# Halving the weight split of one more unit, moving three output steps in a hand-written order, and cutting the first constants' transfer in two

## The reference

```python
n = rmsnorm(x, ln1)
rq, rk, rv, rg, gq, gk, gv, gg, ga, m_r, m_g = split_cols(n @ w_in)
o_r, s_ret = chunked_gated_linear(rotary(rq), rotary(rk) * RET_DK ** -0.5, rv, log_gamma, s_ret)
y_r = (group_rmsnorm(o_r, g_ret) * silu(rg)) @ w_ret_out
log_a = log_sigmoid(ga @ w_gate_up + b_gate_up) / 16
o_g, s_gla = chunked_gated_linear(gq * GLA_DK ** -0.5, gk, gv, log_a, s_gla)
y_g = (group_rmsnorm(o_g, g_gla) * silu(gg)) @ w_gla_out
h = x + (sigmoid(m_r) * y_r + sigmoid(m_g) * y_g) @ w_o
u, vv = split(rmsnorm(h, ln2) @ w_up)
h = h + (gelu(causal_dwconv(u)) * vv) @ w_down
y = rmsnorm(h, ln_f)
```

## Time and profile before

| | |
|---|---|
| median of 3 runs | 823.83 us (823.05, 823.83, 824.13) |
| profiled execution, its own time | 824.17 us |
| its span, from the first to the last instruction | 822.4 us |
| TensorE busy in the span | 812.3 us (99%) |
| VectorE busy | 588.8 us (72%) |
| ScalarE busy | 377.9 us (46%) |
| GpSimd busy | 218.4 us (27%) |
| mean granted TensorE clock | 0.996 of full speed |

### The profile page before, as it was taken

One profiled execution on the slowest core, in us unless ns is written; L12 is line 12 of the kernel. 1 busy time (PEld: TensorE's weight loads), 2 busy tenths in 40 slices (PEclk: granted clock), 3 DMA queues, 4 the chain that ended last, 5 costly groups with the idle time before them and its releaser, 6 DMA issues.

```text
span 822.4 us, 15722 instructions
## 1 busy us (share of the span) xinstructions
PE 812.3 (99%) x6522; PEld 798.8 (97%) x6522; DVE 588.8 (72%) x766; ACT 377.9 (46%) x535; POOL 218.4 (27%) x261
## 2 busy tenths in 40 slices
PE   9999999999999999999999999999999999999996
PEld 9989999999989999999999999999999999999996
DVE  5475669487899786766568877777777756778973
ACT  5653244322456363443244544443444424544574
POOL 4028247343427300000530333333322222000020
PEclk9999999999999999999999999999999999999998
DMA  9769968983328963537996686576677873765622
GB/s 272 220 206 173 270 215 182 202 263 103 110 80 149 231 234 97 186 130 231 199 271 195 142 259 202 150 203 202 241 184 202 231 172 103 202 181 172 175 60 108
DMA packets 163090, 152.32 MB, mean 185 GB/s; under 512 B 6710, under 2 KB 144682, under 8 KB 163005
## 3 DMA queue, kind: packets, MB, share of 16 engines
q1 hardware_dynamic: 129420, 109.73, 42.6%
q0 software_dynamic: 33440, 41.09, 26.6%
q10 hardware_dynamic: 160, 0.53, 0.2%
HBM read 145.36 MB, written 58.40 MB: 248 GB/s over the span
## 4 chain that ended last, share of the span: by engine, by line
PE 95%; DVE 3%; issue 1%; ACT 0%; DVEq 0%
PE mm L2063 52%; PE ax L2371 14%; PE mm L2485 8%; PE ax L2485 6%; PE ax L2084 6%; PE mm L2371 4%; PE ax L2089 2%; PE mm L2146 1%; PE mm L2084 1%; DVE grs L1478 1%; DVE wlo L1468 1%; DVE ysil L1725 0%; DVE ylo L1730 0%; DVE wlo L1742 0%; ACT whi L1030 0%
## 5 line engine op out<-in xcount | busy, mean ns | idle before, releaser
L2063 PE MATMUL mm<-nhi,whi 128*128 128x272 f32 x928 | 196.4, 293 | 0.5 <-DVE wlo L1468 0.5
L2063 PE MATMUL mm<-nhi,wlo 128*128 128x272 f32 x928 | 191.9, 288 | 0.0
L2063 PE MATMUL mm<-nlo,whi 128*128 128x272 f32 x928 | 191.4, 288 | 0.0
L1030 ACT ACTIVATE whi<-raw 128x1024 fp32r<-128x1024 f32 (+2 forms) x111 | 128.2, 1190 | 64.8 <-PE mm L2063 34.7
L2063 PEld LDWEIGHTS mm<-nhi,whi 128*128 128x128 f32 x928 | 146.3, 188 | 3.3 <-DVE wlo L1468 1.0
L2063 PEld LDWEIGHTS mm<-nlo,whi 128*128 128x128 f32 x928 | 145.8, 188 | 0.0
L2063 PEld LDWEIGHTS mm<-nhi,wlo 128*128 128x128 f32 x928 | 145.1, 189 | 0.0
L1742 DVE TENSOR_TENSOR wlo<-raw,whi 128x1024 fp32r<-128x1024 f32 (+1 forms) x78 | 84.4, 1124 | 6.6 <-ACT whi L1030 4.1
L1468 DVE TENSOR_TENSOR wlo<-raw,whi 128x2048 fp32r<-128x2048 f32 x27 | 65.2, 2415 | 13.6 <-ACT whi L1030 13.6
L961 POOL DMA_DIRECT2D v_sums<-in_w_up x24 | 30.8, 4230 | 117.4 <-DVE mlo L1813 116.7
L1030 ACT ACTIVATE whi<-ring 128x1408 fp32r<-128x1408 f32 x25 | 34.6, 1384 | 44.0 <-PE ax L2485 24.0
(11 more groups left out here) (393 smaller groups left out, 1975.2 us busy)
## 6 DMA issues: line engine op xcount, KB each, us to landing
raw<-in_w_in SPq DMA_DIRECT2D x36, 512.0 KB, 4.9
raw<-in_w_up SPq DMA_DIRECT2D x36, 512.0 KB, 6.9
ring<-w_sums SPq DMA_DIRECT2D x16, 704.0 KB, 4.8
w_sums<-in_w_down SPq DMA_DIRECT2D x9, 768.0 KB, 10.6
w_sums<-in_w_down POOLq DMA_DIRECT2D x9, 768.0 KB, 9.6
ring<-in_w_down SPq DMA_DIRECT2D x9, 704.0 KB, 4.7
v_sums<-in_w_up SPq DMA_DIRECT2D x24, 256.0 KB, 7.7
v_sums<-in_w_up POOLq DMA_DIRECT2D x24, 256.0 KB, 14.5
```

The source lines that it names most:

```text
L1030: return act.activation(out, in_, func, **kw).then_inc(done, 1)
L2063: ins = pe.matmul(mm[:, 2 * j + a, 0:HALF], w, x[:, kx, HALF * a:HALF * (a + 1)], start=first and n == 0 and m == 0, stop=last and n == le ...
```

## The change

Three edits. First, unit 3's weights are split as unit 1's were: ACT makes `whi` in two halves of 1024 columns, DVE makes `wlo` in two halves, the first as soon as ACT's first half is there (`half_high`, which takes the place of `hi1_part`). `lo_ready` still comes once, with the second half. Second, `("y2", 2)`, `("y2", 3)` and `("y1", 4)` move from behind block 0 of unit 14 into its block 1, behind `("rn", 2)` and `("ro", 3)` and ahead of `("ri", 2)`. Third, `c1` comes by two transfers: the identity first, the ones and epsilon behind the weights of unit 0, with a semaphore of their own that PE waits for ahead of the first norm's sum.

```diff
+IN_HALVES = (1, 3)
...
-        (14, 0): [("y2", 2), ("y2", 3), ("y1", 4)],
...
-        (14, 1): {1: [("rs", 3)], 2: [("rp", 3)], 4: [("rn", 2), ("ro", 3), ("ri", 2)], 6: [("rx", 3), ("rw", 3), ("rsq", 3), ("y1", 5), ("y2", 4)]},
+        (14, 1): {1: [("rs", 3)], 2: [("rp", 3)], 4: [("rn", 2), ("ro", 3), ("y2", 2), ("y2", 3), ("y1", 4), ("ri", 2)], 6: [("rx", 3), ("rw", 3), ("rsq", 3), ("y1", 5), ("y2", 4)]},
...
-        sp.dma_start(c1[:, :], A["c1"]).then_inc(c1_in, 16)
+        sp.dma_start(c1[:, 0:C1_ONE], A["c1"][:, 0:C1_ONE]).then_inc(c1_in, 16)
...
+        sp.dma_start(c1[:, C1_ONE:C1_N], A["c1"][:, C1_ONE:C1_N]).then_inc(ones_in, 16)
...
-            if s == ("split", 1):
-                act.wait_ge(landed[1], 32)
-                run(whi[1][:, 0:4, :], raw[1][:, 0:4, :], ACT.Copy, hi1_part)
+            if k == "split" and s[1] in IN_HALVES:
+                u = s[1]
+                act.wait_ge(landed[1], 32 * (u // 2 + 1))
+                if u >= 2:
+                    act.wait_ge(filled[1], fills(1, u - 2))
+                run(whi[1][:, 0:4, :], raw[1][:, 0:4, :], ACT.Copy, half_high)
                 run(whi[1][:, 4:8, :], raw[1][:, 4:8, :], ACT.Copy, hi_ready)
...
-            if s == ("split", 1):
-                dve.wait_ge(hi1_part, 1)
+            if k == "split" and s[1] in IN_HALVES:
+                u = s[1]
+                dve.wait_ge(half_high, IN_HALVES.index(u) + 1)
                 st.did(dve.tensor_tensor(wlo[1][:, 0:4, :], raw[1][:, 0:4, :], whi[1][:, 0:4, :].bitcast(F32), ALU.subtract))
-                dve.wait_ge(hi_ready, 2)
+                dve.wait_ge(hi_ready, u + 1)
...
                 pe.wait_ge(acc1_done, 1)
+                pe.wait_ge(ones_in, 16)
                 summed("rstd1", acc)
```

More of the change, by code:

```diff
@@ L409, in build @@
     zeros_ready = sem("zeros_ready")
-    c1_in, c2_in, vec_in, cache_in, rope_in, wg_in = map(sem, ("c1_in", "c2_in", "vec_in", "cache_in", "rope_in", "wg_in"))
+    c1_in, ones_in, c2_in, vec_in, cache_in, rope_in, wg_in = map(sem, ("c1_in", "ones_in", "c2_in", "vec_in", "cache_in", "rope_in", "wg_in"))
     x_in = [sem(f"x_in{j}") for j in range(NJ + 1)]
@@ L415, in build @@
     hi0_part, lo0_part = sem("hi0_part"), sem("lo0_part")
-    hi1_part = sem("hi1_part")
+    half_high = sem("half_high")
     filled = [sem(f"filled{j}") for j in range(2)]
```

## The result

| | before | after |
|---|---|---|
| median | 823.52 us (821.86 to 824.15, 8 runs) | 825.04 us (824.28 to 826.41, 8 runs) |
| ratio, 95% interval | | 1.0023 (1.0015 to 1.0032) |
| profiled execution: own time, span | 824.17, 822.4 us | 824.28, 822.4 us |

The change makes the kernel about 0.2% slower. So I take three distances from each trace: the start of the first product; from there to unit 16's first matmul; from there to the end of the span. Before, these are 11.23, 253.19 (264.42 - 11.23) and 557.98 us (822.4 - 264.42). After, they are 10.44, 254.14 and 557.82 us. The change's places lie in the second distance: 0.95 us longer.

A forecast was written before the change was run, and what follows sets the result against it. TensorE's matrix work, busy 812.3 of 822.4 us, was taken as the bound, with VectorE lacking slack at 264 us. 1.22 - 0.08 + 0 = +1.14 us on 823.83 gave 825.0 us, range 823.1 to 826.1.

The forecast's parts named there:

- First edit, 0.08 kept: Unit 3: the 0.49 us wait for wlo goes, step z starts 0.08 us earlier, the rest is longer waiting ahead of z.
- Third edit, 0: Constants at the start: an earlier identity gains nothing, and the extra issue ahead of unit 1's loads is covered; 0 us.
- Second edit: Units 14 to 16: VectorE, in front of ylo, waits for yhi behind root and rso; unit 16 loses 1.22 us.
- VectorE's gap ended by yhi: Sign ahead of the first moved ylo: VectorE idles about 2.9 us until ACT has made yhi.
- the later reciprocal: VectorE's reciprocal behind the moved steps starts at 247.57 in place of 245.63, 1.94 us later.
- TensorE idle for gsig: Sign ahead of unit 16: TensorE idles about 2 us, waiting for the drain of unit 15's first block.
- The sum was put 0.89 us earlier: Head 2's sum of squares at unit 14: starts at 242.80 in place of 243.69, without TensorE's 0.72 us wait.
- 0.72: Between reciprocal and drain: 0.72 us of the delay vanish in the waits of s0r and wlo and missing overlaps.
- the 0.31 us between unit 16's first two pairs: Start of unit 16: 0.31 in place of 0.25 us was read as the drain already holding TensorE by about 0.06 us.
- no slack there: VectorE at 264 us: each microsecond by which unit 15's first drain moves is a microsecond of the kernel.
- +1.14 us: Sum of all three edits: 1.22 lost at unit 16, less 0.08 at z, plus 0 for the constants.
- The clock falls: Rival at unit 16's new 2.1 us pause: some 6 us at half speed, 3 us more, 828; chance 0.07.

The follow-up runs named there:

- the mended order: Changed kernel with ScalarE's yhi of outputs 2 and 3 at its early place: 821.67 us, ratio 0.9987; this order alone on the kernel before: 822.47 us, 0.9987.
- the pause filled: 14 unread matmuls ahead of unit 16's wait for the drain: with the three steps moved alone 823.83 us, ratio 1.0011; in the changed kernel 823.73 us, 1.0009.
- the changed kernel's second trace: The changed kernel measured once more, unaltered, against the kernel before: 826.00 us, ratio 1.0027.
- moved alone: Only the three moved output steps, on the kernel before: 826.48 us against 822.97, ratio 1.0031.

## Why the prediction came out as it did

The number, 825.0 us, was met (825.04), by a sum that lacked a term.

- **First edit, 0.08 kept:** right. z is 0.10 us earlier against the first product, and the traces with the halves reach unit 16 about 0.1 us earlier than those without (253.08 for 253.19, 252.08 for 252.18). ScalarE's two halves took 1.99 us where the whole took 1.90: 0.09 more, where the row of unit 1 gave 0.10. The estimate from the Trainium skill, page VectorE: DVE Perf Modes, section "The TRN2 errata", was 0.19; the measurement decides.
- **Third edit, 0:** right, by the kernel that has it alone.
- **Second edit:** the mechanism is shown by the mended order, and the signs that were named all came: VectorE's gap ended by yhi, the later reciprocal, TensorE idle for gsig. The sizes are a little off. The sum was put 0.89 us earlier, is 0.99 (with z's share, 0.97 were predicted); the gap ahead of ylo 2.9, is 2.79; the reciprocal 1.94 later, less z's 0.08, is 1.72. From there 0.75 us vanish up to the drain, where I had 0.72. One reading was no evidence: the 0.31 us between unit 16's first two pairs, from which I took that TensorE was held by 0.06, stands in the mended order too (261.63 to 261.94). That VectorE had no slack there is shown by the drain and unit 16 moving together, 0.97 and 0.95 us.
- **The sum:** +1.14 us for the late drain and z together; unit 16 is 0.95 later. With the pause filled, the ratios 1.0009 and 1.0011 give 0.7 and 0.9 us.
- **The step that failed** is the rival "The clock falls", with "Dense work stands on both sides here, so chance 0.07" and 3 us. By the mean clock, it is what happens in 15 of the 17 executions of the changed kernel. Its size was taken from the 6 us at the end of the span; dense work did bring the clock back, after 3.5 us, so it costs 1.5 us. The Trainium skill, page TensorE: Matmul & The Clock Gate, Part 1, says that the throttled state is the default and that activity releases it; the trace agrees, the clock being back at 1.00 from 268.5 us on in the changed kernel's second trace. I had used that rule and then taken the dense neighbours for a protection. With 0.95 us for the drain and 15/17 of 1.5, the loss is near 2.3 us; measured are 1.9 (0.0023 x 823.5) and, again, 2.2 us (0.0027 x 823.1).
- **Why the number held all the same:** partly by chance. The base of the sum, 823.83, was the median of three runs; those of more runs were 823.5, 823.0, 823.1 and 823.6. The drain was 0.2 us too high too. Both made up for a part of the missing clock, and the rest is the draw of the starts: the nine later executions have a median of 826.00 us, all 17 one of 825.15. The forecast of the loss was too small: 0.14% against 0.23% (0.15% to 0.32%) and, again, 0.27%. I had put 0.71 on a change within 0.2%, and by these ratios both are beyond it.

Left open is why one execution keeps its clock through the same 1.9 us pause and another doesn't; the pause has the same length in both. The windows give a hint that was not put to a test. A window's mean clock tells where in it the clock went from 1.00 to 0.50. The changed kernel's second trace, moved alone (two rows), and the profile of the result:

```profile
817.50:818.00 0.50, 0.00 (x0) 0.00 (x0) 0.50 (x2) 0.50 (x1) 0.00 (x0) 0.58 0.00 0
```
```profile
266.00:266.50 0.50, 0.50 (x5) 0.50 (x4) 0.47 (x2) 0.50 (x1) 0.50 (x6) 0.77 1.44 179
819.00:819.50 0.50, 0.00 (x0) 0.00 (x0) 0.50 (x2) 0.50 (x1) 0.00 (x0) 0.73 0.00 0
```
```profile
816.50:817.00 0.50, 0.00 (x0) 0.00 (x0) 0.50 (x2) 0.50 (x1) 0.00 (x0) 0.86 0.00 0
```

In the first, the clock falls at 264.62 us (0.62 in the window shown above), 0.77 behind the pause, and at the end of the kernel at 817.58; in the second at 266.27 and 819.23. Both pairs lie 552.96 us apart. In the third, which kept its clock, the fall at the end is at 816.86, and 552.96 us ahead of it, at 263.90, the pause was still running (it ended at 264.58). So it may be that the clock falls only at moments which the kernel does not set, and that the pause brings it down when such a moment comes after its end. Three traces fit this, and no run was made to test it.

## What to carry to other kernels

A step that is moved in a shared order moves on every engine that has a part in it: the gain was VectorE's (0.99 us), the loss ScalarE's, whose part had been made in idle time; moved on VectorE alone, the same step makes the kernel 0.13% faster. Where TensorE's new wait is longer than any that the kernel had, price a fall of the clock behind it at what dense work needs to bring it back (here 1.5 us), and test it by filling the wait with matmuls that nobody reads. Compare traces by distances between marks, not by spans, when executions start differently.

## What the hardware showed beside that

**The start.** The first product begins between 9.14 and 11.23 us, whichever edits a kernel has. In before, the eight idle matmuls ahead of it took 1.91 us; in the changed kernel, 1.06:

```profile
8.58 1.91 PE L2084 MATMUL mm<-zeros 128*128 128x128 f32 x8
```
```profile
6.75 1.06 PE L2089 MATMUL mm<-zeros 128*128 128x128 f32 x8
...
9.60 1.09 PE L2094 MATMUL ax<-c,x_nat 128*128 128x128 f32 x8 [1.79 <-DMA x_nat<-in_x_prompt]
```

The same matmuls run at about half the rate in one execution, although the granted clock is recorded as 1.00 from 4 to 12 us in both. Where they run faster, TensorE waits for the inputs instead, so that the start gains less than it could.

**The end.** In before, the last matmul ends at 815.40 us and the clock is down within the window at 816.00; with the constants alone, it ends at 813.68 and the clock falls in the window at 816.50:

```profile
816.00:816.50 0.50, 0.00 (x0) 0.00 (x0) 0.40 (x1) 0.42 (x1) 0.00 (x0) 0.64 0.00 0
```
```profile
816.50:817.00 0.50, 0.00 (x0) 0.00 (x0) 0.00 (x0) 0.00 (x0) 0.00 (x0) 0.62 1.02 410
```

So the fall doesn't stand at a fixed distance behind the last matmul: some 0.7 us in the one, 2.9 in the other. That the same pause brings the clock down in one execution and not in another fits this, and is no more than that.
